# A chunked recurrent and attention block on one core: the layers' mixing and second feed-forward products in units of seven half-size products

## The chip, the core and the metric

The kernel runs on one core of one Trainium2 chip, as one program on its engines: TensorE (PE, with its weight loads PEld), VectorE (DVE), ScalarE (ACT), GpSimd (POOL) and SyncE (SP), which here starts the weight transfers. The metric is the device time of one execution in microseconds (us), the median of the runs given.

## What is computed

Two blocks follow each other on 512 tokens of width 1024, all in float32. The first (four recurrent mixers, a routed mixture of 32 experts with 4 per token, a gated embedding) is not touched. The second puts 16 extra rows ahead of the tokens (528 rows) and runs two layers of this form:

```python
for l in range(2):
    ...                                              # retention, pooling, forgetting attention -> o_r, o_p, o_f
    mix = jnp.concatenate([o_r, o_p, o_f], axis=-1)  # 528 x 1024
    mix = jnp.einsum('ble,ed->bld', mix, w_out)      # 1024 x 1024
    h = layer_norm(ALPHA * h + mix, ln1_g, ln1_b)
    a = jnp.einsum('bld,df->blf', h, w1)             # 1024 x 2816
    b = jnp.einsum('bld,df->blf', h, w3)
    y = jnp.einsum('blf,fd->bld', jax.nn.silu(a) * b, w2)   # 2816 x 1024
    h = layer_norm(ALPHA * h + y, ln2_g, ln2_b)
```

The last layer leaves the 16 extra rows out after attention, since the output is the 512 tokens.

## The kernel before

The second block is handled in row groups: "A" is the 16 extra rows (tile 0, called meta) and tiles 1 and 2 of 128 tokens, "B" is tiles 3 and 4. The order of the work on every engine is written out by hand in `layers()`: for each engine the same sequence of calls, `project` (the input products), `attend` (attention, a generator of 22 steps for A and 25 for B, one step at each `each(steps)`), `mix` (the product with `w_out`, then the first layer norm), `feed` (`feed_up`, the products with `w1` and `w3`, and `feed_down`, the product with `w2`, then the second layer norm). While the rows of one group go through `feed`, the attention steps of the next group are dealt out between its products. So `mix` of layer 0, B stands right behind the last `feed_down` of layer 0, A; `mix` of layer 1, A behind that of layer 0, B; and the second `feed_down` of layer 1, A behind `mix` of layer 1, B.

The 2816 inner features are 22 slices of 128, in two chunks of 12 and 10: `feed_up` fills `ff_t` with a chunk, `feed_down` multiplies it by its rows of `w2` and adds into the residual rows `h2`. `mix` and `feed_down` take for each of two column halves and each of two row tiles one product, 8, 12 or 10 slices deep, each slice a matmul of 128 columns by 512 (L1579, L1610), and one narrow product for the meta rows (L1570, L1613). Results go to a ring of three PSUM banks called `main`; DVE adds each to `h2` (L3129, L3191), and behind the last ones normalises the rows: statistics (L2746, L3153), aggregate (L2757, L3163), centre (L2760, L3166), reciprocal, scale (L2764, L3178), with a square root on ACT (L1869) between. PE needs from DVE only that a bank is free again, three results back. Weights come in pieces of 2 MB through a ring of four slots, in the order in which PE asks for them (`weights`).

## Time and profile before

| | |
|---|---|
| median of three runs | 3258.08 us (3255.95 to 3266.2) |
| span of the profiled execution | 3252.7 us, which is 3.25 us under the fastest of the three runs and 5.4 us under their median |
| the layers (from about 1750 us to the end) | 1502 us, PE busy 1482 us |
| mean granted TensorE clock | 0.973 of full speed |

The profile's span runs from the first to the last instruction; what a run's time holds beyond it is the start and end of the program. A program's matmul in float32 shows as two MATMUL records. A record's own time overlaps that of the next, so the pace of a series is read from its start and that of what follows.

### The profile page before, as it was taken

The page shows a single profiled execution, that of the slowest core. Times are in us where ns is not written, and L with a number is a line of the kernel's source. Part 1 is how long each engine was busy: PE and PEld are TensorE (multiplying, and loading weights), DVE is VectorE, ACT ScalarE, POOL GpSimd, SP SyncE. Part 2 cuts the span into 40 slices and gives each one's busy share as a digit, 9 for nine tenths or more (in the row PEclk, how much of TensorE's full clock was granted, in tenths as well). Part 3 has the DMA queues.
Part 4 walks back from the last instruction along what each step waited for, and adds up shares of the span by engine and source line. Part 5 has one row for each costly group of instructions (what it writes and reads, how often), then busy time and mean ns, then how long its engine had stood idle before and what let it go on. Part 6 is the DMA issues. An engine that isn't in the chain of part 4 may idle for free.

```text
span 3252.7 us, 52666 instructions
## 1 busy us (share of the span) xinstructions
PE 3120.2 (96%) x22631; PEld 1747.5 (54%) x22631; DVE 975.8 (30%) x2146; ACT 540.8 (17%) x1129; POOL 47.2 (1%) x58
## 2 busy tenths in 40 slices
PE   9878989999999999999999999999999999999999
PEld 3355545333343333333345668574785758675866
DVE  1633455232223223222363431223023122132101
ACT  1332311111111111111122220130102100040000
POOL 0000002000000000000010000000000000000000
PEclk9888979999999999999989999999999999999999
DMA  9800115999999999999863333234333243243532
GB/s 400 354 1 27 53 53 224 386 410 403 408 397 406 400 406 407 407 407 404 351 251 119 125 130 117 111 143 176 135 126 142 105 194 133 100 176 116 195 145 100
DMA packets 97466, 743.70 MB, mean 229 GB/s; under 512 B 11128, under 2 KB 38336, under 8 KB 57552
## 3 DMA queue, kind: packets, MB, share of 16 engines
q1 hardware_dynamic: 58768, 687.49, 53.6%
q10 hardware_dynamic: 32624, 30.52, 2.9%
q0 software_dynamic: 5968, 24.14, 1.9%
q8 instruction: 83, 1.36, 0.2%
q14 instruction: 23, 0.19, 0.0%
HBM read 674.98 MB, written 67.13 MB: 228 GB/s over the span
## 4 chain that ended last, share of the span: by engine, by line
PE 55%; DMA 28%; DVE 3%; ACT 2%; issue 1%; ACTq 1%; POOL 0%; DVEq 0%
DMA arena<-x_sorted 27%; PE psum L1593 19%; PE psum L1610 9%; PE psum L1540 5%; PE psum L1579 3%; PE psum L1551 3%; PE psum L1244 1%; PE psum L802 1%; ACTq L587 1%; PE psum L1355 1%; PE psum L820 1%; PE psum L1196 1%; PE psum L1319 1%; PE psum L1411 1%; PE psum L1457 1%
## 5 line engine op out<-in xcount | busy, mean ns | idle before, releaser
L1244 PE MATMUL psum<-weight_ring,arena 128*32 128x512 f32 x6192 | 680.8, 594 | 23.6 <-DVE arena L2862 21.7
L1593 PE MATMUL psum<-arena,weight_ring 128*128 128x256 f32 (+1 forms) x2816 | 632.2, 383 | 3.1 <-ACT arena L2226 3.1
L1593 PEld LDWEIGHTS psum<-arena,weight_ring 128*128 128x128 f32 x2816 | 527.6, 189 | 99.0 <-issue 11.0
L1244 PEld LDWEIGHTS psum<-weight_ring,arena 128*32 128x32 f32 x6192 | 199.7, 110 | 485.5 <-issue 464.3
L1319 PE MATMUL psum<-weight_ring,arena 128*32 128x256 f32 x6144 | 338.2, 380 | 0.0
L1610 PE MATMUL psum<-weight_ring 128*128 128x512 f32 x704 | 305.4, 593 | 4.2 <-DVE weight_ring L3149 4.2
L1319 PEld LDWEIGHTS psum<-weight_ring,arena 128*32 128x32 f32 x6144 | 196.6, 110 | 153.0 <-issue 26.8
L1610 PEld LDWEIGHTS psum<-weight_ring 128*128 128x128 f32 x704 | 132.9, 190 | 169.3 <-issue 162.5
L2884 DVE STREAM_TRANSPOSE arena<-arena 128x384 f32<-128x384 f32 x32 | 18.6, 580 | 630.8 <-DMA arena<-x_sorted 630.8
L3149 DVE TENSOR_TENSOR weight_ring<-weight_ring,psum 128x256 f32<-128x256 f32 (+1 forms) x88 | 37.5, 426 | 486.1 <-PE psum L1593 480.3
L1540 PE MATMUL psum<-weight_ring,arena 128*128 128x512 f32 (+2 forms) x512 | 170.0, 489 | 3.1 <-ACT arena L2226 3.1
L818 PE MATMUL psum<-arena,weight_ring 128*128 128x512 f32 x288 | 134.2, 617 | 10.9 <-DMA weight_ring<-weights 6.6
L1540 PEld LDWEIGHTS psum<-weight_ring,arena 128*128 128x128 f32 x512 | 96.0, 190 | 70.5 <-issue 59.8
L2273 ACT ACTIVATE weight_ring<-psum 128x256 f32<-128x256 f32 (+1 forms) x88 | 34.1, 387 | 513.2 <-PE psum L1593 513.0
L1551 PE MATMUL psum<-arena,weight_ring 128*128 128x272 f32 (+1 forms) x512 | 117.1, 387 | 0.0
L2103 ACT ACT_TABLE_LOAD x32 | 41.1, 1283 | 428.0 <-issue 428.0
L1579 PE MATMUL psum<-weight_ring,arena 128*128 128x512 f32 x256 | 110.6, 592 | 0.0
L1551 PEld LDWEIGHTS psum<-arena,weight_ring 128*128 128x128 f32 x512 | 95.9, 189 | 19.1 <-issue 2.0
L818 PEld LDWEIGHTS psum<-arena,weight_ring 128*128 128x128 f32 x288 | 54.5, 196 | 76.8 <-issue 67.2
L3191 DVE SCALAR_TENSOR_TENSOR arena<-arena,psum 128x512 f32<-128x512 f32 x32 | 22.1, 690 | 232.5 <-PE psum L1610 232.5
L820 PE MATMUL psum<-weight_ring,arena 128*128 128x512 f32 (+1 forms) x192 | 90.8, 601 | 0.0
L2109 ACT COPY arena<-psum 128x256 f32<-128x256 f32 x96 | 36.0, 375 | 293.2 <-PE psum L1319 280.0
(435 smaller groups left out, 2532.0 us busy)
## 6 DMA issues: line engine op xcount, KB each, us to landing
weight_ring<-exp_gu SPq DMA_DIRECT2D x129, 2048.0 KB, 11.9
weight_ring<-weights SPq DMA_DIRECT2D x104, 2048.0 KB, 7.8
weight_ring<-exp_down SPq DMA_DIRECT2D x64, 2048.0 KB, 11.5
x_sorted<-arena SPq DMA_DIRECT2D x2, 10752.0 KB
arena<-x_sorted ACTq DMA_DIRECT2D x132, 96.0 KB, 21.6
y_sorted<-arena ACTq DMA_DIRECT2D x128, 96.0 KB, 17.6
y_sorted<-arena SPq DMA_DIRECT2D x2, 5632.0 KB, 39.7
y_sorted<-arena SPq DMA_DIRECT2D x2, 5120.0 KB, 37.3
```

Of the source, the lines that this page charges most:

```text
L818: mm = pe.matmul(bank, w[:, k, a:a + P], x_t[:, k, :], start=(k == 0), stop=(k == KT - 1))
L820: mm = pe.matmul(bank[:, 0:width], x_t[:, k, t * P:(t + 1) * P], w[:, k, a:a + width], start=(k == 0), stop=(k == KT - 1))
L1244: mm = pe.matmul(psum[j * GROUP:(j + 1) * GROUP, g, :], xg[:, k // 4, g, k % 4 * GROUP:(k % 4 + 1) * GROUP], w[:, kk, j * 512:(j + 1) * 51 ...
L1319: mm = pe.matmul(psum[j * GROUP:(j + 1) * GROUP, 3 + g, 0:256], hid_t[:, g, k * GROUP:(k + 1) * GROUP], w[:, kk, j * 256:(j + 1) * 256], s ...
L1540: mm = pe.matmul(bank[:, 0:width], h2_t[:, k, OFF[t]:OFF[t] + P], w[:, k, 0:width], start=first, stop=last)
L1551: mm = pe.matmul(bank[:, 0:b - a], w[:, k, c:c + P], h2_t[:, k, a:b], start=first, stop=last)
L1579: mm = pe.matmul(bank, h2_t[:, k, OFF[t]:OFF[t] + P], ws[half][0][:, k, :], start=(k == 0), stop=(k == KT - 1))
L1593: mm = pe.matmul(bank[:, 0:b - a], w[:, k, col:col + P], h2_t[:, k, a:b], start=(k == 0), stop=(k == KT - 1))
L1610: mm = pe.matmul(bank, ff_t[:, f, OFF[t] - a:OFF[t] - a + P], w[:, half * 512:(half + 1) * 512], start=first, stop=last)
L2103: T.did(act.activation(sig[:, g, :], swi[:, g, 0:256], ACT.Sigmoid, scale=SWIGLU_ALPHA), swish_given)
L2109: T.did(act.copy(y_out[:, g, :], psum[:, 3 + g, 0:256]), y_drained)
L3149: V.did(dve.tensor_tensor(g, g, bank[:, 0:b - a], ALU.mult), main.drained["v"])
```

## The change

`mix` and `feed_down` become one function, `fast`, called 16 times (the list `FAST`). The features are cut in three chunks of 8, 8 and 6 slices instead of 12 and 10, so a unit has two row tiles (`t` and `first`), two column halves, and two halves of the depth of `depth` = 4 slices (3 in the last chunk). A unit makes its 2x2 blocks from seven products of `depth` matmuls where there were eight. For this, GpSimd forms the weight differences `b12 - b11` (in `fast_t1`) and `b22 - b12` (in place of b12), DVE forms four sums or differences of the left operand and two of the weights (`b11`, `b21` in place), ACT copies one product out of its bank, and DVE adds partial results together and to `h2`. The 16 meta rows keep their ordinary product, now ahead of the seven. One attention step stands ahead of the meta product and in each of the places 0, 2, 4 and 6 of a unit. The layer norm's parts of the last unit stand between and behind its additions. The lists of `layers()` keep their order with three chunks. Some buffers and semaphores move and a scratch area for GpSimd's transfers shrinks to 4096 bytes a partition to make room for the new tiles.

```diff
@@ -113,13 +113,27 @@
 ROW_CHUNKS = ((0, 512), (512, 512), (1024, 256), (1280, 256))
-FF_CHUNKS = ((0, 12), (12, FT))
+FF_CHUNKS = ((0, 8), (8, 16), (16, FT))
...
+FAST = [("mix", 0, "A", 0), ("down", 0, "A", 0), ("down", 0, "A", 1), ("down", 0, "A", 2),
+        ("mix", 0, "B", 0), ("down", 0, "B", 0), ("down", 0, "B", 1), ("down", 0, "B", 2),
+        ("mix", 1, "A", 0), ("down", 1, "A", 0), ("down", 1, "A", 1), ("mix", 1, "B", 0), ("down", 1, "A", 2),
+        ("down", 1, "B", 0), ("down", 1, "B", 1), ("down", 1, "B", 2)]
+STEP_SLOTS = (0, 2, 4, 6)
...
+    return KT // 2 if name == "mix" else (FF_CHUNKS[c][1] - FF_CHUNKS[c][0]) // 2
...
+            def fast(u, operand, ready, ready_late, steps):
+                name, l, x, c = FAST[u]
+                depth = fast_depth(name, c)
+                t, first = fast_tiles(x)
+                def rows(k, tile):
+                    return operand[:, k, OFF[tile] - operand_from(name, l, x):OFF[tile] - operand_from(name, l, x) + P]
+                def product(bank, lhs, rhs, start=True):
+                    for k in range(depth):
+                        mm = pe.matmul(bank, lhs(k), rhs[:, k, :], start=start and k == 0, stop=(k == depth - 1), skip_group_check=True)
+                    return mm
+                at = W_OUT if name == "mix" else W_DOWN + 2 * c
+                wa, at_a = weights(l, at)
+                if has_meta(l, x):
+                    wb, at_b = weights(l, at + 1)
+                    ready()
+                    ready_late(META)
+                    if name == "down":
+                        each(steps)
+                    bank = main.bank(pe)
+                    for k in range(2 * depth):
+                        w = (wa, wb)[k // depth].rearrange("p k n -> p (k n)").rearrange("p (k n) -> p k n", k=4)[:, k % depth, :]
+                        for j in range(4):
+                            mm = pe.matmul(bank[32 * j:32 * j + META, 0:256], operand[:, k, 0:META], w[:, j * 256:(j + 1) * 256],
+                                           start=(k == 0), stop=(k == 2 * depth - 1), skip_group_check=True)
+                    main.ship(mm, ("fast", u, "meta"), "v")
+                    fast_meta[u] = main.done()
+                else:
+                    ready()
+                    at_b = None
+                if 0 in STEP_SLOTS:
+                    each(steps)
+                bank_p1 = main.reserve(pe, 0)
+                if at_b is None:
+                    fast_at[u] = (at_a, at_a + 1)
+                else:
+                    fast_at[u] = (at_a, at_b)
+                b11, b12, b21, b22 = fast_views(u)
+                product(bank_p1, lambda k: rows(k, t), b11).then_inc(part_filled, 1)
+                if 1 in STEP_SLOTS:
+                    each(steps)
+                bank_p7 = main.reserve(pe, 2)
+                pe.wait_ge(sums_ready, 8 * u + 2)
+                pe.wait_ge(diffs_ready, 3 * u + 3)
+                product(bank_p7, lambda k: rows(k, first), b12).then_inc(part_filled, 1)
+                if 2 in STEP_SLOTS:
+                    each(steps)
+                if at_b is None:
+                    wb, at_b = weights(l, at + 1)
+                    assert at_b == at_a + 1
+                ready_late(P)
+                pe.wait_ge(part_copied, u + 1)
+                mm = product(bank_p1, lambda k: rows(depth + k, t), b21, False)
+                main.ship(mm, ("fast", u, "c11"), "v")
+                if 3 in STEP_SLOTS:
+                    each(steps)
+                bank_p6 = main.reserve(pe, 0)
+                pe.wait_ge(sums_ready, 8 * u + 5)
+                mm = product(bank_p6, lambda k: fast_s2[:, k, :], b11)
+                main.ship(mm, ("fast", u, "p6"), "v")
+                if 4 in STEP_SLOTS:
+                    each(steps)
+                bank_p5 = main.reserve(pe, 1)
+                product(bank_p5, lambda k: fast_s1[:, k, :], fast_t1).then_inc(part_filled, 1)
+                if 5 in STEP_SLOTS:
+                    each(steps)
+                pe.wait_ge(sums_ready, 8 * u + 7)
+                mm = product(bank_p7, lambda k: rows(depth + k, first), b21, False)
+                main.ship(mm, ("fast", u, "c21"), "v")
+                piece_free[at_a] = main.done()
+                if 6 in STEP_SLOTS:
+                    each(steps)
+                pe.wait_ge(sums_ready, 8 * u + 8)
+                mm = product(bank_p5, lambda k: fast_s4[:, k, :], b22, False)
+                main.ship(mm, ("fast", u, "c12"), "v")
+                piece_free[at_b] = main.done()
...
+            def differences(u):
+                name, l, x, c = FAST[u]
+                depth = fast_depth(name, c)
+                b11, b12, b21, b22 = fast_views(u)
+                if u:
+                    pool.wait_ge(part_filled, 3 * u)
+                at_a, at_b = fast_at[u]
+                pool.wait_ge(layer_landed[at_a % LAYER_SLOTS], layer_count(at_a))
+                pool.tensor_tensor(fast_t1[:, 0:depth, :], b12, b11, ALU.subtract).then_inc(diffs_ready, 1)
+                pool.wait_ge(diffs_ready, 3 * u + 1)
+                pool.wait_ge(layer_landed[at_b % LAYER_SLOTS], layer_count(at_b))
+                if u in fast_meta:
+                    pool.wait_ge(*fast_meta[u])
+                for part in (slice(0, depth // 2), slice(depth // 2, depth)):
+                    pool.tensor_tensor(b12[:, part, :], b22[:, part, :], b12[:, part, :], ALU.subtract).then_inc(diffs_ready, 1)
...
+                for n in range(7):
+                    if n in STEP_SLOTS:
+                        each(steps)
+                    if n == 0:
+                        act.wait_ge(part_filled, 3 * u + 1)
+                        A.did(act.copy(fast_u2, main.peek(("fast", u, "c11"))), part_copied)
...
+                    dve.wait_ge(*main.drained_of(("mix", l, t)))
+                V.settle()
+                fast(FAST.index(("mix", l, x, 0)), h2_t, iter(()), sem("mid_ready"), landed)
...
+                V.settle()
+                then(dve.tensor_tensor(s1, rows(0, first), rows(1, first), ALU.add), sums_ready)
+                V.did(dve.tensor_tensor(rows(0, first), rows(0, t), rows(0, first), ALU.subtract), sums_ready)
+                then(dve.tensor_tensor(s2, s1, rows(0, t), ALU.subtract), sums_ready)
+                V.did(dve.tensor_tensor(s4, rows(1, t), s2, ALU.subtract), sums_ready)
+                if 0 in STEP_SLOTS:
+                    each(steps)
+                dve.wait_ge(diffs_ready, 3 * u + 3)
+                dve.wait_ge(part_filled, 3 * u + 1)
+                then(dve.tensor_tensor(b11, b22, t1, ALU.subtract), sums_ready)
+                if 1 in STEP_SLOTS:
+                    each(steps)
+                if 2 in STEP_SLOTS:
+                    each(steps)
+                add(t, 0, main.take(dve, ("fast", u, "c11")), scale, main.drained["v"])
+                V.did(dve.tensor_tensor(b21, b21, b11, ALU.subtract), sums_ready)
+                if ready is not None:
+                    V.settle_other(main.drained["v"])
+                    half_stats(t, 0)
+                if 3 in STEP_SLOTS:
+                    each(steps)
+                bank = main.take(dve, ("fast", u, "p6"))
+                dve.wait_ge(part_copied, u + 1)
+                then(dve.tensor_tensor(fast_u2, fast_u2, bank, ALU.add), main.drained["v"])
+                dve.wait_ge(part_filled, 3 * u + 2)
+                then(dve.tensor_tensor(fast_u3, fast_u2, main.peek(("fast", u, "c21")), ALU.add), sums_ready)
+                add(t, 1, fast_u2, scale)
+                add(first, 0, fast_u2, scale)
+                add(first, 1, fast_u3, scale)
+                V.settle()
+                if 4 in STEP_SLOTS:
+                    each(steps)
+                dve.wait_ge(part_filled, 3 * u + 3)
+                add(first, 1, main.peek(("fast", u, "c12")), 1.0, sums_ready)
+                if ready is not None:
+                    V.settle()
+                    half_stats(first, 1)
+                if 5 in STEP_SLOTS:
+                    each(steps)
+                add(first, 0, main.take(dve, ("fast", u, "c21")), 1.0, main.drained["v"])
+                if ready is not None:
+                    V.settle()
+                    dve.wait_ge(sem("layer_ln_landed"), 16 * landed)
+                    half_stats(first, 0)
+                    centered = norm_centered(first)
+                if 6 in STEP_SLOTS:
+                    each(steps)
+                add(t, 1, main.take(dve, ("fast", u, "c12")), 1.0, main.drained["v"])
+                V.settle()
+                if ready is not None:
+                    norm_scaled(centered, ready, parts)
+                    half_stats(t, 1)
+                    norm_scaled(norm_centered(t), ready, parts)
+                    if has_meta(l, x):
+                        half_stats(0, 0)
+                        half_stats(0, 1)
+                        norm_scaled(norm_centered(0), ready, parts)
+
```

Three places show what the engines now run. First PE at `mix` of layer 0, B, right behind the last `feed_down` of layer 0, A. Before, L1613 is the narrow product of the down unit, L1579 the mix:

```order
L1613 MATMUL psum<-weight_ring 16x256 [waits main_drained_dve]
L1613 MATMUL psum<-weight_ring 16x256 x39
L1579 MATMUL psum<-weight_ring,arena 128x512 [waits fox_outs_drained,layer_weights_landed_1,main_drained_act,main_drained_dve,fox_turns_drained_dve,fox_turns_drained_act]
L1579 MATMUL psum<-weight_ring,arena 128x512 x6
L1579 MATMUL psum<-weight_ring,arena 128x512 [waits fox_outs_drained]
L1579 MATMUL psum<-weight_ring,arena 128x512 [waits main_drained_dve]
L1579 MATMUL psum<-weight_ring,arena 128x512 x7
L1579 MATMUL psum<-weight_ring,arena 128x512 [waits main_drained_dve,layer_weights_landed_2]
L1579 MATMUL psum<-weight_ring,arena 128x512 x7
L1579 MATMUL psum<-weight_ring,arena 128x512 [waits main_drained_dve]
L1579 MATMUL psum<-weight_ring,arena 128x512 x7
```

And with the change, the last rows of the unit of depth 3 and the first of the mix unit (L1620 is every product of a unit):

```order
L1620 MATMUL psum<-weight_ring 128x512 [waits fast_sums_ready]
L1620 MATMUL psum<-weight_ring 128x512 x2
L1620 MATMUL psum<-weight_ring,arena 128x512 [waits fast_sums_ready]
L1620 MATMUL psum<-weight_ring,arena 128x512 x2
L1620 MATMUL psum<-weight_ring,arena 128x512 [waits main_drained_act,fox_turns_drained_dve,main_drained_dve,fox_turns_drained_act,start_landed_1]
L1620 MATMUL psum<-weight_ring,arena 128x512 x3
L1620 MATMUL psum<-weight_ring,arena 128x512 [waits fast_diffs_ready,fast_sums_ready,main_drained_dve]
L1620 MATMUL psum<-weight_ring,arena 128x512 x3
L1620 MATMUL psum<-weight_ring,arena 128x512 [waits fast_part_copied,fox_outs_drained,start_landed_2]
L1620 MATMUL psum<-weight_ring,arena 128x512 x3
```

The second product of the mix unit now waits for DVE's sums and GpSimd's differences; before, a mix product waited for a free bank only.

Second, DVE at the same place, with the change. L3332 are additions to `h2`, L3292 to L3314 the layer norm, L3343 and L3344 the first two sums of the mix unit, which let PE's second product go:

```order
L3314 SCALAR_TENSOR_TENSOR arena<-arena 128x1024 [waits vector_step]
L3292 BN_STATS arena<-arena 128x6 [waits layer_start]
L3299 BN_AGGR arena<-arena 128x2 [waits vector_step]
L3302 SCALAR_TENSOR_TENSOR arena<-arena 128x1024 [waits variance_ready]
L3311 RECIPROCAL arena<-arena 128x1 [waits root_ready]
L3314 SCALAR_TENSOR_TENSOR arena<-arena 128x1024 [waits vector_step]
L3292 BN_STATS arena<-arena 16x6 [waits layer_start]
L3292 BN_STATS arena<-arena 16x6
L3299 BN_AGGR arena<-arena 16x2 [waits vector_step]
L3302 SCALAR_TENSOR_TENSOR arena<-arena 16x1024 [waits variance_ready]
L3311 RECIPROCAL arena<-arena 16x1 [waits root_ready]
L3314 SCALAR_TENSOR_TENSOR arena<-arena 16x1024 [waits vector_step]
L3343 TENSOR_TENSOR arena<-arena 128x512 [waits layer_start,main_drained_act]
L3344 TENSOR_TENSOR arena<-arena 128x4x128 [waits fast_sums_ready]
```

The norms of tile 1 (scale), tile 2 and the meta rows stand ahead of the sums that the mix unit begins with; before, no sums followed.

Third, PE in the second down unit of layer 1, A, with the change, from place 4 on (the last of these rows begins the product behind it). L1509, L854, L1537 and L1544 are an attention step:

```order
L1620 MATMUL psum<-weight_ring,arena 128x512 x3
L1509 MATMUL psum<-weight_ring,arena 64x128 [waits fox_outs_drained,fox_turns_drained_act]
L1509 MATMUL psum<-weight_ring,arena 64x128 x9
L854 MATMUL psum<-arena,weight_ring 16x128 [waits fox_turns_drained_act,fox_weights_ready]
L854 MATMUL psum<-arena,weight_ring 128x128 x3
L854 MATMUL psum<-arena,weight_ring 16x128 [waits fox_turns_drained_act]
L854 MATMUL psum<-arena,weight_ring 128x128 x3
L1537 MATMUL psum<-arena 128x512 [waits score_drained_dve]
L1537 MATMUL psum<-arena 128x512
L1544 MATMUL psum<-arena 128x16 [waits fox_turns_drained_act] x2
L1620 MATMUL psum<-arena 128x512 [waits main_drained_dve]
```

A step that waits for `fox_weights_ready` (DVE's work on the scores of the step before) now stands two products of 4 matmuls behind that step; before, two of 8 or one of 12 or 10.

## Rows read from the trace of the kernel before

**Rows 1.** Page: share of the span; 40 slices, tenths busy.
```profile
PE 3120.2 (96%) x22631; PEld 1747.5 (54%) x22631; DVE 975.8 (30%) x2146; ACT 540.8 (17%) x1129; POOL 47.2 (1%) x58
...
PEclk9888979999999999999989999999999999999999
```
**Rows 2.** Windows of the layers: busy us of each engine (count), granted clock, DMA.
```profile
1950.00:2240.00 290.00, 287.68 (x1382) 198.15 (x1385) 72.59 (x139) 51.91 (x99) 0.00 (x0) 1.00 0.30 113
2240.00:2350.00 110.00, 109.63 (x639) 68.76 (x632) 21.18 (x35) 12.85 (x41) 1.06 (x2) 1.00 0.50 192
sum 1502.00, PE 1482.30 PEld 1022.16 DVE 365.10 ACT 235.99 POOL 2.66; mean PE 211.76 PEld 146.02 DVE 52.16 ACT 33.71 POOL 0.38
```
**Rows 3.** PE's timeline around a mix: start, us, instruction, count [idle before].
```profile
1902.04 27.63 PE L1579 MATMUL psum<-weight_ring,arena 128*128 128x512 f32 x64
1929.60 3.69 PE L1570 MATMUL psum<-weight_ring,arena 128*16 128x128 f32 x128
...
2201.73 34.60 PE L1610 MATMUL psum<-weight_ring 128*128 128x512 f32 x80 [0.53 <-DVE weight_ring L3149]
2236.26 4.51 PE L1613 MATMUL psum<-weight_ring 128*16 128x256 f32 x80
```
**Rows 4.** DVE groups in the layers by shape: count, busy us, mean ns.
```profile
L3191 DVE SCALAR_TENSOR_TENSOR arena<-arena,psum 128x512 f32<-128x512 f32 x32 | 22.1, 690 | 232.5 <-PE psum L1610 232.5
L3061 DVE TENSOR_TENSOR weight_ring<-psum,weight_ring 128x1024 f32<-128x1024 f32 x6 | 7.3, 1225 | 10.0 <-PE psum L1485 10.0
L2942 DVE TENSOR_TENSOR arena<-arena 128x384 f32<-128x384 f32 x8 | 4.5, 558 | 0.3
L3195 DVE SCALAR_TENSOR_TENSOR arena<-arena,psum 16x256 f32<-16x256 f32 x8 | 3.3, 416 | 4.9 <-PE psum L1613 4.6
```
**Rows 5.** GpSimd groups of the whole span.
```profile
L1799 POOL COPY arena<-arena 128x1024 f32<-128x1024 f32 x4 | 4.2, 1061 | 530.7 <-DVE arena L2764 530.7
```
**Rows 6.** DVE's timeline, norm of tile 2 and the meta rows.
```profile
2237.17 0.69 DVE L3153 BATCH_NORM_STATS2 arena<-arena 128x6 f32<-128x512 f32 x1
2237.90 0.21 DVE L3163 BATCH_NORM_AGGREGATE arena<-arena 128x2 f32<-128x12 f32 x1
2238.14 1.29 DVE L3166 SCALAR_TENSOR_TENSOR arena<-arena 128x1024 f32<-128x1024 f32 x1
2239.54 1.29 DVE L3178 SCALAR_TENSOR_TENSOR arena<-arena 128x1024 f32<-128x1024 f32 x1
2242.71 1.27 DVE L3153 BATCH_NORM_STATS2 arena<-arena 16x6 f32<-16x512 f32 x2
```
**Rows 7.** Timeline of one attention step's chain, 2112 to 2121 us.
```profile
2113.11 1.13 PE L1485 MATMUL psum<-arena 64*128 64x512 f32 x4
2114.29 1.23 DVE L3061 TENSOR_TENSOR weight_ring<-psum,weight_ring 128x1024 f32<-128x1024 f32 x1 [1.51 <-PE psum L1485]
2119.24 0.90 DVE L3084 TENSOR_SCALAR weight_ring<-weight_ring,arena 128x528 f32<-128x528 f32 x2
```
**Rows 8.** PE's timeline in the first block, between two idle times.
```profile
1654.82 1.58 PE L802 MATMUL psum<-arena 128*128 128x128 f32 x8 [2.70 <-DVE arena L2902]
1676.85 1.98 PE L1340 MATMUL psum<-weight_ring,arena 128*128 128x512 f32 x4 [2.28 <-DVE arena L2917]
```
**Rows 9.** Windows of 5 us around these.
```profile
1640.00:1645.00 5.00, 5.00 (x6) 1.41 (x5) 2.07 (x3) 0.00 (x0) 3.76 (x4) 0.50 0.97 408
...
1655.00:1660.00 5.00, 4.32 (x12) 2.37 (x12) 3.94 (x6) 4.04 (x5) 3.82 (x4) 0.53 1.02 406
1660.00:1665.00 5.00, 5.00 (x11) 2.14 (x10) 4.89 (x5) 0.00 (x0) 0.00 (x0) 0.79 0.71 284
1675.00:1680.00 5.00, 3.15 (x8) 1.48 (x9) 4.45 (x7) 1.49 (x2) 0.00 (x0) 1.00 0.62 203
```
**Rows 10.** Timeline of the end of the kernel.
```profile
3245.72 0.69 DVE L3191 SCALAR_TENSOR_TENSOR arena<-arena,psum 128x512 f32<-128x512 f32 x1 [4.16 <-PE psum L1610]
3248.81 1.42 DVE L3178 SCALAR_TENSOR_TENSOR arena<-arena 128x512 f32<-128x512 f32 x2
```

264 lines of the change are left out of this document (130 added, 134 removed).

## The prediction

> **What bounds the kernel now.** The page comes first: PE is busy 96% of the span, DVE 30%, POOL 1%, and the granted clock of TensorE is at its upper level in almost all slices behind the first block [rows 1]. The windows of the layers say the same of the part that is changed: 1482 of 1502 us busy at clock 1.00, with DVE at 365 us and POOL at 2.7 us [rows 2]. So in the layers the time is PE's work, and what PE waits for there now is about 20 us, some 6 of them behind its last product. PE's timeline shows that the work is dense: the 64 records of the mix of layer 0, A take from 1902.04 to 1929.60 us, 27.56 us or 0.431 us a record, and the 80 records of a down chunk from 2201.73 to 2236.26, again 0.431, across four banks and without idle time; idle time stands only ahead of the first, 0.53 us, where PE waits for DVE's last product into `ff_t` [rows 3]. A matmul 128 by 512 in float32 is two records, so 0.861 us.
>
> **What is taken away.** Twelve units have depth 4 (four mixes, eight down chunks), four have depth 3. Each makes seven products of its depth where there were eight, so 12 x 4 + 4 x 3 = 60 matmuls or 120 records go: 120 x 0.4306 = 51.7 us. The narrow meta products hold the same columns: a mix had 128 records of 128 columns in 3.7 us, now 64 of 256, and a record of 256 takes 4.51 / 80 = 0.056 us, 3.6 us [rows 3]. Nothing gained there.
>
> **What a plain unit costs on the other engines.** DVE had four additions of 0.69 us. Now it has, at depth 4, four sums of 512 elements, two of 2048 and nine additions. An operation on 384 elements takes 0.56 us and one on 1024 takes 1.23, a slope of 1.04 ns an element [rows 4], so 512 take 0.69 and 2048 take 2.29 us (an estimate from these rows). The sum is 4 x 0.69 + 2 x 2.29 + 9 x 0.69 = 13.6 us, against 28 x 0.861 = 24.1 us of PE. It fits in total; what counts is each hand-over. With t = 0 at PE's first product and 3.45 us a product: the two sums for the second product are ready at 1.5 (needed 3.45); b11 at 5.9, behind the first product (needed 10.3); DVE takes the third product at 10.5, then b21 until 13.5, and the fourth at 14.0, so `fast_u3` is there at 15.4 (needed 17.2); the addition of the fifth ends at 18.1 (needed 20.7). None is late. At depth 3 a product is 2.58 us, and with the statistics of 0.69 us between [rows 6] `fast_u3` comes at 12.4 (needed 12.9) and the last sum at 15.2 (needed 15.5): just in time, with no room. GpSimd's differences are made while `feed_up` runs, where POOL is idle. I book nothing for the hand-overs; if each of the four units of depth 3 missed both by 0.5 us, that would be 4 us.
>
> **What comes on the path.** (a) The norms. At three places a unit follows directly behind one that ends in a layer norm, and its second product needs two sums that stand behind all of it in DVE's order. From the rows, statistics 0.69, aggregate 0.21, centre until scale 1.40, scale 1.29 and gaps make 3.8 us for a tile, and 4.3 for the meta rows, whose two statistics take 1.27 [rows 6]. Behind the end of PE's last product in layer 0, A, DVE needs 1.65 for the last addition (it comes late from the centring), 1.5 for the scale of the first tile, 3.8, 4.3, and 1.5 for the two sums: 12.75 us. PE covers 3.45 with its first product: 9.3 us idle at mix 0, B. At mix 1, A there are no meta rows behind: 5.0. At the last down chunk of layer 1, A, behind mix 1, B, it is 0.9 + 1.5 + 3.8 + 1.2 = 7.4 less 2.6: 4.8. Together 19.1 us. The cover that these norms had, PE's products into three banks, is what the new wait removes.
> (b) The meta units. The differences for b12 may start only behind the meta product, and the second product needs them. No row has a GpSimd operation with two inputs. The nearest is its copy of 1024 elements, 1.06 us [rows 5]; below, two such pieces take 2.1 us and hide under the 3.45; above, I take each input at a copy's time, 2.12 us a piece, 4.7 with hand-overs, so 1.3 us idle, and 1.0 at depth 3 (pieces of 512 and 1024). I take the upper end, since two operands must be read: 2.3 us for the two meta units that have no attention step to cover it. Both ends differ by 2 us only.
> The Trainium skill, "GPSIMD Engine Reference", section "Elementwise — side-by-side cycle accounting", gives 4497 ns for a `tensor_tensor` of 2048 float32 elements against 2293 ns on DVE. By that the two waits would be 2.9 us and not 2.3. No run shows the former yet; the latter agrees with 2.29 from the slope of rows 4.
> (c) Attention steps. A step's scores end at 2114.24 on PE, DVE and ACT work on them until 2120.14, 5.9 us [rows 7], and the step after it needs the result. `feed_up` has two products of 3.8 us and PE's own part of a step, 2.5 us, between, so it hides there. In a unit two products of 3.45 stand between, but DVE puts its sums ahead of the step. Where heavy steps fall in a unit (steps 21 to 23 in the second chunk of layer 0, A, and 20 to 23 in that of layer 1, A), I get 1.7 + 1.0 and 1.4 us. The other units with steps hold light ones, under 1 us of DVE each: nothing. Together 4.1 us.
> (d) A third chunk adds four waits at a chunk's start of 0.53 us [rows 3]: 2.1.
> (e) The end. From DVE's last addition at 3245.72 to its last scale at 3250.23 are 4.5 us [rows 10]. Now the scale of the first tile and the late last addition stand in between: 2.4 more.
> (f) The clock. Behind an idle time of 2.70 us at 1652 us the granted clock shows 0.53 and 0.79 in two windows of 5 us, that is the lower level, 1.2 GHz, for some 6 us; behind one of 2.28 us it stays at 1.00 [rows 8, 9]. The first costs 5 x 0.47 + 5 x 0.21 = 3.4 us of full speed, about 3.2 of it outside the wait. I take that for each of the three waits of (a), 9.6 us, and none for those under 2 us. Below: nothing. Above: 12 us at the lower level as at 1640 us [rows 9], 6 us each.
> The sum is -51.7 + 19.1 + 2.3 + 4.1 + 2.1 + 2.4 + 9.6 = **-12.1 us**. The span is 3252.7 us, so 3240.6; its difference to the median, 5.4 us, stays, and the median goes from 3258.1 to **3246 us**. The likeliest case's own range is 3237 to 3255.
>
> **The rivals.** Waits and clock are mild (chance 0.2): no drop of the clock behind waits of 5 us, and part of the norm hidden; -51.7 + 30.0 = -21.7 or a little under, 3236 us. For it speaks that the clock at 1.00 survived 2.28 us; against it that 2.70 us did not.
> The clock turns it round (0.14): each of the seven waits, the short ones too, is followed by 12 us at the lower level, as the window at 1640 us has it behind a row of short gaps. 7 x 6 = 42 in place of 9.6: -51.7 + 30.0 + 42 = +20, 3278 us. It decides from 3.1 us a wait on (21.7 / 7). Against it: in the layers PE is dense on both sides of each wait.
> The two engines collide (0.12): GpSimd's differences run beside DVE's sums with two inputs in the meta units and at the norms. If both took twice as long there, b12 would come some 4.5 us later in two units and the sums and norms at mix 0, B and mix 1, A about 2 us later: +11 to +13, so no change, 3259 us. The profile has no moment at which both work on such operations. The Trainium skill, "GPSIMD Engine Reference", section "Key points", says that GpSimd shares its SBUF interfaces with VectorE and contends with DVE instructions with two SBUF inputs; it gives no size.
> More waits than I see (0.09): the hand-overs in the units of depth 3 and the step units cost 1 us each in 10 units, 3256 us.
>
> **How the numbers follow.** My own case has 0.45. This measurement can't tell a change under about 0.3%, 9.8 us: faster is under 3248.3, slower over 3267.9. My case ends faster in about three of four (0.34 of 0.45), the rest within; the mild one is faster (0.2); the collision and the added waits lie within, with a fifth of them on either side; the clock case is slower. That makes faster 0.56, same 0.27, slower 0.17. The range runs from under the mild case, 3230, to 3272, which leaves out most of the clock case and a tail below.
>
> **What will show it.** L1620 with 28 x 12 + 21 x 4 = 420 matmuls, 840 records at 0.431 us, where L1579 and L1610 had 960. PE idle ahead of the second product at mix 0, B by 9 us, at mix 1, A and the last chunk of 1, A by 5, released by DVE's L3344; the granted clock behind them. POOL's L1953 at 2.1 us or 2.3 a piece. DVE's L3351 at 2.29 us. I am wrong if PE is idle for more than 35 us more than before in the layers (then the hand-overs are not hidden), or for less than 20 (then the norms are covered by something that I missed).

## The result, and the profile after

The changed kernel takes 3276.81 us (median of 11 runs, 3271.49 to 3284.14) against 3264.88 us for the kernel before, run beside it: a ratio of 1.0043, 95% interval 1.0033 to 1.0054. It is 0.43% slower, some 14 us (the two medians alone are 11.9 us apart, 0.37%). The forecast was 3246 us. Of the 30.8 us between forecast and measurement, 6.8 are the kernel before itself, which took 3264.88 us beside the changed one and 3258.08 us in the three runs that the forecast started from.

The first rows of the page of the changed kernel (its profiled execution spans 3282.3 us), which answer to [rows 1]:

```profile
PE 3083.7 (94%) x22447; PEld 1726.7 (53%) x22447; DVE 1186.1 (36%) x2338; ACT 551.2 (17%) x1146; POOL 190.5 (6%) x106
...
PEclk9888889899999999999989999998999999999999
```

PE has 36.5 us less to do over the whole span, and the kernel is slower. The windows from the layers' first load to the end, first of the kernel before and then of the changed one (length, busy us of PE, PEld, DVE, ACT and POOL with counts, granted clock, DMA), split that:

```profile
1740.40:3252.70 1512.30, 1491.90 (x6919) 1026.82 (x6917) 365.10 (x748) 237.16 (x563) 8.56 (x17) 1.00 0.37 138
```
```profile
1751.60:3282.30 1530.70, 1467.12 (x6735) 1012.90 (x6733) 575.80 (x940) 247.87 (x580) 149.15 (x65) 0.98 0.37 136
```

The layers are 18.4 us longer in this pair of profiles. PE's idle time in them went from 20.4 us (1512.30 less 1491.90) to 63.6: **+43.2**, where 30.0 was forecast. PE's busy time fell by 24.8 us and not by 51.7: at most 26.9 us of what was removed was given back to a lower clock, where 9.6 was forecast (the granted clock, weighed by PE's busy time in windows of 0.5 us, gives 25.2). 43.2 and 26.9 less 51.7 make 18.4.

PE's timeline of the changed kernel (start, us, instruction, count, idle time before it) through the end of the last unit of layer 0, A and through mix 0, B, where most of this lies:

```profile
2243.16 7.08 PE L1620 MATMUL psum<-weight_ring 128*128 128x512 f32 x12 [2.10 <-DVE weight_ring L3344]
2250.09 2.74 PE L1620 MATMUL psum<-weight_ring,arena 128*128 128x512 f32 x6
...
2261.64 9.05 PE L1620 MATMUL psum<-weight_ring,arena 128*128 128x512 f32 x14 [3.66 <-DVE arena L3332]
2279.05 13.16 PE L1620 MATMUL psum<-weight_ring,arena 128*128 128x512 f32 x24 [8.36 <-issue]
2292.05 3.60 PE L1620 MATMUL psum<-arena 128*128 128x512 f32 x8
```

The 8.36 us ahead of mix 0, B's second product are the norm wait that was forecast at 9.3. The 3.66 us were not forecast at all. Six records take 2.74 us at the full clock, and the 12 behind the first wait take 7.08 where two such groups would take 5.4. The windows of 5 us there show the clock fall to its lower level (0.50 of 2.4 GHz is 1.2 GHz) behind each of these waits:

```profile
2260.00:2265.00 5.00, 3.36 (x4) 1.51 (x5) 4.83 (x7) 0.29 (x1) 4.92 (x3) 0.54 0.88 364
...
2275.00:2280.00 5.00, 0.95 (x1) 0.50 (x2) 4.67 (x7) 0.40 (x1) 0.56 (x1) 0.50 0.19 67
2280.00:2285.00 5.00, 5.00 (x8) 2.09 (x7) 2.48 (x2) 0.00 (x0) 0.00 (x0) 0.57 0.34 143
2285.00:2290.00 5.00, 5.00 (x13) 2.19 (x12) 1.11 (x2) 0.00 (x0) 0.00 (x0) 1.00 0.00 0
```

What kept PE waiting for 3.66 us stands in the timelines of POOL and of DVE, here around the twin of that wait in layer 0, B:

```profile
2631.28 4.83 POOL L1947 TENSOR_TENSOR arena<-weight_ring 128x2048 f32<-128x2048 f32 x1 [29.91 <-PE psum L1620]
...
2636.18 4.98 POOL L1953 TENSOR_TENSOR weight_ring<-weight_ring 128x1024 f32<-128x1024 f32 x2
```
```profile
2631.66 4.99 DVE L3332 SCALAR_TENSOR_TENSOR arena<-arena,weight_ring 128x512 f32<-128x512 f32 x1
2636.69 0.69 DVE L3332 SCALAR_TENSOR_TENSOR arena<-arena,psum 128x512 f32<-128x512 f32 x1
2637.41 0.70 DVE L3292 BATCH_NORM_STATS2 arena<-arena 128x6 f32<-128x512 f32 x1
...
2639.70 2.55 DVE L3302 SCALAR_TENSOR_TENSOR arena<-arena 128x1024 f32<-128x1024 f32 x1
```

An addition of 512 elements that takes 0.69 us elsewhere took 4.99. It began 0.4 us behind POOL's subtraction and ended at 2636.65, half a microsecond behind POOL's end at 2636.11. The next, with its second input in PSUM, and the statistics, with one input, run at their own time although POOL is busy again; the centring, which reads two inputs from SBUF (1.29 us in [rows 6]), again takes 2.55, and ends 1.1 us behind POOL's second piece. The same thing reaches out of the units: POOL's first difference is released as soon as its weights land, 50 us ahead of the first unit, and falls on an attention step:

```profile
1863.06 4.51 POOL L1947 TENSOR_TENSOR arena<-weight_ring 128x2048 f32<-128x2048 f32 x1 [105.56 <-DMA weight_ring<-weights]
```
```profile
1863.97 3.65 DVE L3225 TENSOR_TENSOR weight_ring<-weight_ring,arena 16x32 f32<-16x32 f32 x1
```
```profile
1871.41 1.36 PE L854 MATMUL psum<-arena,weight_ring 16*16 16x16 f32 x6 [2.65 <-DVE weight_ring L3235]
```

That addition of 16 by 32 took 0.18 us in the kernel before:

```profile
1852.72 0.18 DVE L3074 TENSOR_TENSOR weight_ring<-weight_ring,arena 16x32 f32<-16x32 f32 x1
```

In the changed kernel it ends at 1867.62, POOL's instruction at 1867.57, and PE stands idle for 2.65 us that were not there.

Outside the layers the two programs do the same work, but the two profiled executions differ by 11.2 us where the layers begin. The last issue of the scatter on POOL and the first load of sorted rows on ACT are 7.1 us apart before and 27.6 in the changed kernel's profile; here both engines' timelines of the latter:

```profile
563.71 0.96 POOL L1911 DMA_INDIRECT x_sorted<-arena  x1 [0.30 <-issue]
```
```profile
591.33 1.85 ACTq L613 DMA_DIRECT2D arena<-x_sorted  x4
```

So the study had three questions: what holds DVE, what the low clock costs, and whether the scatter belongs to the change (the compile argument for the scratch area was changed with it, and the prediction gave it no price).

### The profile page after: what moved, and what is told of

Same layout as the page of the kernel before. It is cut to its first block, busy times and chain, and to the rows that moved or that the text cites. A ratio compares the mean times of both kernels' runs of the same rounds, so it can differ in the third digit from the quotient of the medians.

```text
span 3282.3 us, 52707 instructions
## 1 busy us (share of the span) xinstructions
PE 3083.7 (94%) x22447; PEld 1726.7 (53%) x22447; DVE 1186.1 (36%) x2338; ACT 551.2 (17%) x1146; POOL 190.5 (6%) x106
## 4 chain that ended last, share of the span: by engine, by line
PE 51%; DMA 28%; DVE 6%; issue 2%; ACT 2%; ACTq 1%; POOL 1%; DVEq 0%
DMA arena<-x_sorted 26%; PE psum L1713 19%; PE psum L1620 10%; PE psum L1592 5%; PE psum L1603 3%; PE psum L854 1%; PE psum L1296 1%; PE psum L1371 1%; PE psum L1407 1%; ACTq L613 1%; PE psum L1248 1%; PE psum L872 1%; PE psum L1463 1%; DMA x_sorted<-arena 1%; PE psum L1509 1%
## 5 line engine op out<-in xcount | busy, mean ns | idle before, releaser
L1620 PE MATMUL psum<-weight_ring,arena 128*128 128x512 f32 x368 | 176.6, 632 | 22.3 <-issue 12.6
L1620 PE MATMUL psum<-weight_ring 128*128 128x512 f32 x352 | 162.7, 611 | 11.3 <-issue 8.6
L1620 PEld LDWEIGHTS psum<-weight_ring,arena 128*128 128x128 f32 x368 | 73.8, 203 | 118.1 <-issue 108.3
L1592 PEld LDWEIGHTS psum<-weight_ring,arena 128*128 128x128 f32 x512 | 96.0, 190 | 70.5 <-issue 59.8
L1947 POOL TENSOR_TENSOR arena<-weight_ring 128x2048 f32<-128x2048 f32 (+1 forms) x16 | 68.6, 4286 | 1033.1 <-DMA weight_ring<-weights 958.3
L1620 PEld LDWEIGHTS psum<-weight_ring 128*128 128x128 f32 x352 | 66.9, 194 | 95.9 <-issue 94.8
```

Of the source, the lines that this page charges most:

```text
L1592: mm = pe.matmul(bank[:, 0:width], h2_t[:, k, OFF[t]:OFF[t] + P], w[:, k, 0:width], start=first, stop=last)
L1620: mm = pe.matmul(bank, lhs(k), rhs[:, k, :], start=start and k == 0, stop=(k == depth - 1), skip_group_check=True)
L1947: pool.tensor_tensor(fast_t1[:, 0:depth, :], b12, b11, ALU.subtract).then_inc(diffs_ready, 1)
```

## The experiments

Ratios are to the kernel before, on the same chip; 1 to 4, 5 to 8, 9 with 10, and 11 were run beside it on four occasions. The changed kernel gave 1.0043 and 1.0042 on two of them, the two edits of 4 gave 0.9948 and 0.9962, so a difference of 0.15% between ratios of two occasions says little. "Layers" is the time from the layers' first load to the end of the span, in one profile each; in two executions of one program it differs by some 3 us (1530.7 and 1528.1, 1497.1 and 1499.7), and between the two kernels without the units that differ only in the scratch area by 4.7.

**1. The scratch area alone.**

```diff
-    nc = bacc.Bacc("TRN2", target_bir_lowering=False, num_devices=1)
+    nc = bacc.Bacc("TRN2", target_bir_lowering=False, num_devices=1, dynamic_dma_scratch_size=4096)
```

> The kernel before with one argument changed: the compile argument that sets the scratch area for software-made DMA descriptors to 4096, as in the changed kernel; no instruction moves. Theory A (the smaller area makes the scatter of the sorted rows land late): from the first of the 16 indirect issues to the first load of sorted rows about 48 us instead of 27.8, and the kernel 15 to 21 us (0.45 to 0.65 %) slower than before. Rival B (the scatter's 20.6 us in the changed kernel's trace have another cause, such as where the expert weights' loads fell in that run): about 28 us again, and the time within 0.3 % of before.

Measured: 0.9989 (0.9976 to 1.0002). The first load of sorted rows came 27.75 us after the first indirect issue (547.00 to 574.75). Theory A is wrong. The changed kernel profiled once more (experiment 5) has 27.8 us as well. In 13 profiles, nine of them with the small area and the changed units, the 48 us occur once; what caused them there stays open, and the change is not it. Where the layers begin varies by more than that wait would explain: between 1732.4 and 1751.6 us over these profiles, and at 1749.1 in experiment 5 without it. The layers of this run are 1517.0 us with 20.4 us idle, as before; the 4 us between them are the clock. It dipped at two places where it had not in the profile of before, once behind the very wait of 2.18 us that stands in both, once behind one of 0.70 us that stands in both. So some 4 us of a difference between two profiles can be that.

**2. POOL's differences in short instructions.**

```diff
-                pool.tensor_tensor(fast_t1[:, 0:depth, :], b12, b11, ALU.subtract).then_inc(diffs_ready, 1)
+                for k in range(depth):
+                    last = pool.tensor_tensor(fast_t1[:, k:k + 1, :], b12[:, k:k + 1, :], b11[:, k:k + 1, :], ALU.subtract)
+                last.then_inc(diffs_ready, 1)
...
-                for part in (slice(0, depth // 2), slice(depth // 2, depth)):
-                    pool.tensor_tensor(b12[:, part, :], b22[:, part, :], b12[:, part, :], ALU.subtract).then_inc(diffs_ready, 1)
+                for k in range(depth):
+                    last = pool.tensor_tensor(b12[:, k:k + 1, :], b22[:, k:k + 1, :], b12[:, k:k + 1, :], ALU.subtract)
+                last.then_inc(diffs_ready, 2)
```

> The changed kernel, with the weight differences on POOL cut into instructions of 512 columns (four of them, or three, where one had 2048 or 1536). Theory A (a DVE instruction whose inputs are both in SBUF does not start until the POOL instruction that is running has ended, so its length is what hurts): the DVE instruction that took 3.65 us instead of 0.18 ahead of the first unit, and the three additions that took 6.20 us instead of 2.1 in the last unit of a feed, come down to little more than their own time; PE's wait of 2.65 us at the first difference and its two of 3.66 us go, with the low clock behind the first; 8 to 16 us faster than the changed kernel as it is. Rival B (POOL holds the DVE off across consecutive instructions as well, or both run slower side by side in proportion): the same total hold, no gain, within 3 us of the changed kernel or slower by the added instructions.

Measured: 0.9983 (0.9967 to 0.9999), some 0.6% under the changed kernel. The layers take 1509.8 us, 20.9 less than in the changed kernel's profile; 57.2 of them idle, 6.4 less, and 1452.6 busy, 14.5 less. The POOL and DVE timelines of this kernel at the first difference:

```profile
1851.74 5.13 POOL L1948 TENSOR_TENSOR arena<-weight_ring 128x512 f32<-128x512 f32 x4 [105.44 <-DMA weight_ring<-weights]
```
```profile
1852.66 0.38 DVE L3228 TENSOR_TENSOR weight_ring<-weight_ring,arena 16x32 f32<-16x32 f32 x1
...
1853.18 1.33 DVE L3228 TENSOR_TENSOR weight_ring<-weight_ring,arena 128x256 f32<-128x256 f32 x1
```

DVE gets in between two pieces: the hold is 0.2 and 0.9 us (1.33 against 0.40) instead of 3.5, and both 3.66 us waits and the 2.65 us one are gone. Theory A holds, and the gain is above the 8 to 16 us that it gave. The four pieces take 5.13 us instead of 4.51, which nothing waits for here. Most of the gain is the clock: short waits went, and with them the slow products behind them. What grew is the norm waits, since PE now arrives earlier at them: 10.32, 6.82 and 5.63 us at the three places, 22.8 in all against 19.0.

**3. The sums ahead of the norm.** The four activation sums of mix 0B, mix 1A and down 1A chunk 2 are called from within the unit before, ahead of its `norm_scaled`:

```diff
+                if u + 1 in EARLY:
...
+                    fast_sums(u + 1)
                 if ready is not None:
                     norm_scaled(centered, ready, parts)
```

> The changed kernel, with the four activation sums of the units that follow a norm (mix 0B, mix 1A, down 1A chunk 2) computed ahead of the rest of that norm. Theory A (the norms of the unit before are what keeps PE waiting there): PE's idle times of 8.36, 4.26 and 6.33 us ahead of those units' second products go, and with them the low clock of the products around them (13 us for 24 records instead of 10.3); 15 to 20 us faster than the changed kernel. Rival B (the norm then ends 2 to 3 us later, and the row transposes that read it are late instead): less than half of that comes back, the rest stands as a longer wait at the start of the next projection or of the next feed.

Measured: 0.9994 (0.9982 to 1.0007), 16 us under the changed kernel. The layers take 1514.6 us, 53.3 idle. Theory A holds in the main, though not all the waits go: mix 0, B's second product no longer waits, but ACT's copy does, since it is queued behind the square roots of the same norm. PE's timeline of this kernel:

```profile
2242.10 12.46 PE L1621 MATMUL psum<-weight_ring,arena 128*128 128x512 f32 x22 [3.66 <-DVE arena L3348]
2258.77 5.46 PE L1621 MATMUL psum<-weight_ring,arena 128*128 128x512 f32 x6 [4.21 <-ACT weight_ring L2417]
```

So 8.36 became 4.21 there; at mix 1, A 0.84 us are left of 4.26, and at the last chunk of 1, A 1.47 and 0.90 of 6.33. The hold of 3.66 us is untouched.

**4. Both edits.**

> The changed kernel with both edits: POOL's differences in instructions of 512 columns, and the sums of three units ahead of the norm's rest. If both theories A hold and their gains add, 25 to 35 us faster than the changed kernel, near 3245 us; if either rival B holds, what the other edit alone gives. The scatter's 20 us stay in either case, if they come from the scratch area.

Measured: 0.9948 (0.9929 to 0.9966), 3240.93 us. They nearly add: 0.95% under the changed kernel, where the edits alone gave 0.60 and 0.49. The layers take 1497.1 us, 33.6 less than in the changed kernel, 48.5 idle. This is within the 25 to 35 us that both theories A gave. What now stands ahead of the second product at mix 0, B and mix 1, A is POOL, whose short pieces and DVE's sums keep each other waiting (four pieces take 7.14 us there instead of 5.13, and three of DVE's four sums 1.63 to 1.75 us instead of 0.69); PE's timeline of this kernel:

```profile
2246.41 4.07 PE L1621 MATMUL psum<-weight_ring,arena 128*128 128x512 f32 x5 [3.90 <-POOL weight_ring L1956]
```

**5. The changed kernel again.**

> The changed kernel once more, unaltered, with a new profile. Theory A (the scatter's 48 us from the first indirect issue to the first load of sorted rows belong to that one execution): about 28 us in this profile, a span near 3270, and the layers again 18 us longer than before; the ratio to before stays at 1.004. Rival B (something in the changed program makes it so in each execution): 48 us again.

Measured: 1.0042 (1.0026 to 1.0059). The layers take 1528.1 us with 63.9 idle, so the layers' part of the result repeats, and the scatter's does not. One of the waits that the hold makes did not bring the low clock this time; PE's timeline and the windows behind it (granted clock 1.00 in both):

```profile
1870.31 0.93 PE L854 MATMUL psum<-arena,weight_ring 16*16 16x16 f32 x6 [2.46 <-DVE weight_ring L3235]
```
```profile
1870.00:1875.00 5.00, 4.69 (x25) 3.57 (x26) 2.13 (x5) 4.26 (x13) 0.00 (x0) 1.00 0.86 360
1875.00:1880.00 5.00, 5.00 (x39) 3.69 (x38) 3.13 (x11) 1.42 (x7) 0.00 (x0) 1.00 0.25 56
```

**6. Three more edits at the same three units.** In PE the order of the second and third product is turned round at these units, ACT's copy goes ahead of the roots, and the meta rows' norm of layer 0 goes behind mix 0B's weight difference:

```diff
+                if u not in EARLY:
+                    second()
...
                 main.ship(mm, ("fast", u, "c11"), "v")
+                if u in EARLY:
+                    second()
...
+                    if u + 1 in EARLY:
+                        copy_first(u + 1)
...
+                if u == 4:
+                    half_stats(0, 0)
+                    half_stats(0, 1)
+                    norm_scaled(norm_centered(0), sem("layer_start"))
```

> Both edits (POOL's differences in instructions of 512 columns; the sums of three units ahead of the norm) and three more at those units: PE takes the product that needs no weight difference second, ACT's copy of the first product stands ahead of the square roots of the norm, and the norm of the meta rows of layer 0 follows behind mix 0B's last weight difference. Theory A (PE's 3.90 us for POOL, 2.61 us for ACT and 0.82 us for DVE in mix 0B, 3.89 us in mix 1A, and 1.46 and 0.90 us in down 1A chunk 2 are the order of three queues, and nothing else is late behind them): 6 to 11 us faster than with the two edits alone, near 0.992 of before. Rival B (the wait moves: the meta rows' norm is late for the next projection, or the second product waits for POOL all the same): less than 4 us.

Measured: 0.9965 (0.9952 to 0.9979), so no gain over the two edits alone. The waits named are gone, but 4.26, 4.25 and 2.08 us came in their place ahead of the next product. DVE's timeline of this kernel says who is late, the sum of weights (L3383) that stands behind the second tile's norm:

```profile
2264.01 1.29 DVE L3334 SCALAR_TENSOR_TENSOR arena<-arena 128x1024 f32<-128x1024 f32 x1
2265.60 2.29 DVE L3383 TENSOR_TENSOR weight_ring<-weight_ring,arena 128x2048 f32<-128x2048 f32 x1 [0.30 <-DVE arena L3334]
```

Rival B, in a form of its own: the wait moved by one product.

**7. A third chunk with ordinary products.** The kernel before, with `FF_CHUNKS = ((0, 8), (8, 16), (16, FT))` and two weight pieces a chunk.

> The kernel before with nothing but the feed-forward chunks changed: three of 8, 8 and 6 blocks instead of 12 and 10, each with the ordinary product, and the attention steps spread over them. Theory A (a third chunk costs little: a wait of about 0.6 us at its start in four feeds, and an add more per chunk on a DVE that is not the bound): 2 to 4 us slower than before, within 0.3 %. Rival B (the attention steps bunch at the new borders and cost waits as they do in the changed kernel, 4.4 us ahead of the second unit of layer 0 and 5.0 in layer 1): 8 to 12 us slower; then the third chunk and not the half-size products accounts for most of what the scheme failed to give.

Measured: 1.0013 (1.0001 to 1.0025); layers 1515.2 us, 20.9 idle. Theory A: the third chunk costs 3 to 4 us by these two numbers, and not the 8 to 12 of rival B. Of the layers' 2.9 us, 1.7 are a drop of the clock that the other profile lacks.

**8. One POOL instruction in the kernel before**, with the small scratch area, and a buffer of its own that POOL clears at the start.

```diff
+                if free is None:
+                    at = mark["mix"]
+                    pool.wait_ge(sem("zeros_ready"), 2)
+                    pool.wait_ge(layer_landed[at % LAYER_SLOTS], 16 * (at // LAYER_SLOTS + 1))
+                    pool.tensor_tensor(spare[:, 0:2048], spare[:, 0:2048], spare[:, 0:2048], ALU.subtract)
```

> The kernel before (with the scratch area of 4096) and one POOL instruction more, a subtraction of 128x2048 on a buffer of its own that nothing reads, released when mix 0A's first weights have landed, where the changed kernel has its first weight difference. Theory A (a DVE instruction whose inputs are both in SBUF is held until POOL's has ended): the 16x32 DVE addition that is due beside it takes up to 3.7 us instead of 0.18, PE waits 2 to 3 us behind it and runs slower for some 10 us: 3 to 6 us more up to mix 0A (0.1 to 0.2 %). Rival B (it was not the instruction but the weights it read, which PE or a transfer used as well): no DVE instruction longer than before, no wait.

Measured: 1.0016 (1.0005 to 1.0027), against 0.9989 for the same kernel without the instruction, on another occasion. Its POOL, DVE and PE timelines:

```profile
1850.66 3.59 POOL L1839 TENSOR_TENSOR spare<-spare 128x2048 f32<-128x2048 f32 x1 [105.42 <-DMA weight_ring<-weights]
```
```profile
1851.51 2.79 DVE L3082 TENSOR_TENSOR weight_ring<-weight_ring,arena 16x32 f32<-16x32 f32 x1
```
```profile
1858.10 0.92 PE L803 MATMUL psum<-arena,weight_ring 16*16 16x16 f32 x6 [1.60 <-DVE weight_ring L3092]
```

POOL's instruction ends at 1854.25, the addition at 1854.30, for 0.18 us of work. Nothing else reads its buffer, so rival B (the weights that it read) is out: the instruction itself holds DVE. PE waited 1.60 us, less than the 2 to 3 expected, and the window of 5 us behind it shows the clock at 0.70, 1.5 us more: 3 us in all, the lower end of what theory A gave. That this dip belongs to the wait isn't shown: the profile of experiment 1, without the instruction, has one of the same size some 15 us later in the layers, and both profiles' layers take 1517.0 us. So what experiment 8 shows is the hold and the wait, and not what they cost.

**9. The sum of weights ahead of the second norm**, on top of 6.

> The kernel of e6_best with one thing moved: at its three units the sum of weights that the third product reads (it stood behind the second tile's norm on DVE) stands ahead of that norm. In e6_best PE waited 4.26, 4.25 and 2.08 us for it. Theory A (DVE's order is all that was late): these go, and nothing else comes in their place: 7 to 10 us faster than e6_best, 5 to 8 faster than the two edits alone. Rival B (the norm that is now 2.3 us later, or the halves of the norm's rows that the turn of rows reads, makes the next projection wait): under 4 us faster than e6_best.

Measured: 0.9947 (0.9929 to 0.9966), 3236.9 us; layers 1493.0 us, 45.2 idle, the shortest of all. The waits of 6 went in mix 1A (4.25 to 0.85) and in down 1A (2.08 to 0.73), while mix 0B kept 4.64 us, for the addition that is queued behind the meta rows' norm. Compared with 6 the layers are 7.8 us shorter, within the 7 to 10 of theory A; but only 2.2 of it are idle time, and 3.4 are two drops of the clock in the profile of 6, behind waits of 0.69 and 2.55 us that stand in both and left the clock up in 9. So the edit is worth less than theory A had.

**10. The two edits once more, on the same chip as 9.**

> The kernel of e4_both once more, beside e9_wsum on one chip. The layers from their first product to their last should again take 1326 us (what the order of the queues sets repeats to a microsecond), and the ratio to before again about 0.995; if the ratio moves by more than 0.3 %, the difference between e4_both and e6_best is one between chips and says nothing of their edits.

Measured: 0.9962 (0.9949 to 0.9974). From the first product of the first unit to the last product of the last one 1328.9 us, against 1326.1 in experiment 4. The ratio moved by 0.14%, under the 0.3% that the expectation had set. The interval overlaps that of 9; that 9 is better than 4 is read from the layers (1493.0 against 1497.1 and 1499.7, of which 45.2 against 48.5 and 47.0 idle) and not from the ratios, and is 2 to 3 us besides the clock.

**11. The meta rows' norm later still.**

```diff
                 add(first, 0, main.take(dve, ("fast", u, "c21")), 1.0, main.drained["v"])
+                if u == 4:
+                    half_stats(0, 0)
+                    half_stats(0, 1)
+                    norm_scaled(norm_centered(0), sem("layer_start"))
```

> The kernel of e9_wsum with the norm of layer 0's meta rows put later inside mix 0B: behind the last addition of the third result instead of behind the weight difference. In e9_wsum it takes 4.3 us of DVE at 2263 and PE waits 4.64 us for the addition queued behind it. Theory A (that norm can hide in the gap that DVE has ahead of the last result): the 4.64 us go and mix 0B with the chunk ahead of it takes 52 to 53 us instead of 56.95; 3 to 5 us faster than e9_wsum. Rival B (the next projection's turn of the meta rows waits for it): a wait of 2 us or more at the start of the projection of layer 1, and less than 3 us gained.

Measured: 0.9978 (0.9963 to 0.9994), and layers of 1506.3 us with 55.0 idle: a loss against 9. The 4.64 us went and the stretch took 51.3 us, as theory A has it. But the loader of the next norm's parameters waits for this norm, and its transfer lands 10 us after the issue. The POOL, DVE and PE timelines of this kernel:

```profile
2274.56 0.56 POOL L1944 DMA_DIRECT2D arena<-ln_mid  x1 [22.08 <-DVE arena L3334]
```
```profile
2272.79 1.27 DVE L3334 SCALAR_TENSOR_TENSOR arena<-arena 16x1024 f32<-16x1024 f32 x1
2284.51 0.69 DVE L3312 BATCH_NORM_STATS2 arena<-arena 128x6 f32<-128x512 f32 x1 [10.45 <-DMA arena<-ln_mid]
```
```profile
2287.52 2.90 PE L855 MATMUL psum<-arena 128*128 128x128 f32 x16 [13.97 <-DVE arena L3374]
```

Neither theory had this: rival B looked for a wait in the right place, but for another reason.

The layers of all profiles by their windows (us, one profile each; the last column is the clock's shortfall from 1.00, summed over windows of 5 us):

| kernel | layers | PE busy | PE idle | clock lost |
|---|---|---|---|---|
| before | 1512.3 | 1491.9 | 20.4 | 1.7 |
| 1, small scratch area | 1517.0 | 1496.6 | 20.4 | 5.5 |
| 7, three plain chunks | 1515.2 | 1494.3 | 20.9 | 3.6 |
| 8, one POOL instruction | 1517.0 | 1495.1 | 21.9 | 5.8 |
| changed / again (5) | 1530.7 / 1528.1 | 1467.1 / 1464.2 | 63.6 / 63.9 | 33.1 / 29.7 |
| 2, short POOL instructions | 1509.8 | 1452.6 | 57.2 | 17.8 |
| 3, sums ahead of the norm | 1514.6 | 1461.3 | 53.3 | 23.6 |
| 4 / 10, both | 1497.1 / 1499.7 | 1448.6 / 1452.8 | 48.5 / 47.0 | 7.7 / 12.8 |
| 6, three more edits | 1500.8 | 1453.4 | 47.4 | 11.1 |
| 9, sum of weights early | 1493.0 | 1447.8 | 45.2 | 5.9 |
| 11, meta norm later | 1506.3 | 1451.3 | 55.0 | 16.2 |

Over the two profiles of either kernel the units make the layers 11 to 18 us longer (1528.1 and 1530.7 against 1512.3 and 1517.0), which agrees with the 14 us of the result.

## Why the prediction was wrong

The direction was wrong, and by its own terms two steps failed.

**The step that failed first: the place of the collision between the two engines.** The prediction held it as a rival at 0.12, priced at 11 to 13 us, looked for it in the meta units and at the norms, and let both engines take twice as long. What the runs show is no sharing but a hold: a DVE instruction with both inputs in SBUF does not get through until POOL's instruction ends, whatever its own size (0.18 us became 3.65, and 2.79 in experiment 8). So its price goes by the length of POOL's instruction (holds of 3.5 and 4.3 us beside instructions of 4.51 and 4.83), and it strikes wherever POOL happens to start. The differences "made while `feed_up` runs, where POOL is idle" were booked at nothing because POOL was idle; DVE was not. At 1863 us it hit an attention step. In the two feeds of layer 0 the next mix's difference started beside the last additions of the depth 3 unit (3.66 us each). In the second chunk of 0, A, PE's wait for an attention step was 3.87 us, and 1.71 once POOL's instructions were short, so about the 1.7 forecast was the step's own and the rest the hold. The Trainium skill, "SBUF — State Buffer", section "Who interferes with whom", states that the contention is an exclusive lock, that a DVE instruction with two SBUF inputs contends with a GpSimd instruction that reads SBUF, and that one with at most one SBUF input (outside of DVE's two-port modes) does not. The trace agrees, with the addition of 4.99 us and the one beside it, from PSUM, at 0.69. The prediction had cited only the page that gives no size, and made the collision proportional. By experiment 2, which only cuts POOL's instructions, the holds cost 0.6% or about 20 us; by the profiles 6.4 us of idle time (10 to 12 us of waits less, the norm waits 3.8 longer) and 14.5 of busy time.

**The second: (f), the clock.** It booked 3.2 us behind each of three waits and none for the others. Low clock shows behind ten: 2.65, 2.33, 3.87, 2.10, 3.66, 8.36, 3.66, 4.26, 6.33 and 2.76 us, each with 1.7 to 5.1 us of full speed lost, 3.1 in the mean, 30.7 in all, 25.2 of it in PE's busy time. The price was about right and the number of waits was not: seven of the ten are the holds, the meta units and the last feed, which the sum had at nothing or under 2 us. How long the wait is doesn't settle it alone. In the layers of all thirteen profiles, each of the 36 waits of 2.75 us or more was followed by a stretch at the lower clock; of the 20 between 2.0 and 2.7 us nine were and eleven were not, the same wait of the same program among both (2.46 us in experiment 5, 2.65 in the first profile; 2.10 us in both); and five more such stretches began behind waits of 0.51 to 0.70 us, and one behind 1.60. This is the rival in which the clock turns it round, with its direction right, and its price per wait twice what was measured, for more waits than it had; that its 3278 us lie next to the 3276.81 is luck. About half of the loss fell out of the first failure: with the holds gone (2) it is 17.8 us, with the norms out of the way too (4) 7.7, or 12.8 in the second profile (10). Of the 33.6 us between the changed kernel and experiment 4, 15.1 are idle time and 18.5 are products that ran faster.

**What held.** (a) The norms: 8.36, 4.26 and 6.33 us, together 18.95, against 9.3, 5.0 and 4.8, together 19.1. Experiment 3 shows that this is DVE's order, and that the same norm also holds ACT's copy. (e) The end: from PE's last product to the end 7.1 us before (the prediction read some 6) and 9.0 after, +1.9 against 2.4. (d) The third chunk: experiment 7 gives about 3 us against 2.1. The plain units of depth 4 have no hand-over waits: the first two units of the last feed take 24.28 us each to the end of their last record, against 24.1 in the working. So the prediction's own sign, more than 35 us of added idle time, did come true, but not for the reason that it gave there (hand-overs inside the units that are not hidden). The 51.7 us are there nearly whole: in experiment 9 PE's busy time is 44.1 us less, and the clock took 3.2 back in busy time, so 47.3 were removed; in the changed kernel 24.8 and 25.2 make 50.0. The rest was not traced.

**Terms that were mis-sized.** (b) The two meta units cost 2.33 and 2.10 us, 4.4 against 2.3. POOL's pieces of 1024 take 2.41 us in the mean, above the upper end of 2.12 that was taken, but in the second the hold also stands in it (DVE's first sum took 2.33 us instead of 0.56). (c) In 1, A the attention step cost 0.32 us, not 1.4. A wait at the start of the last feed grew from 1.11 to 2.76 us; it was not in the list, and its cause was not traced.

So the sum as it should have read: some 50 removed; 30 us of waits as forecast, some 13 more, 12 of them holds of DVE by POOL; and 25 us, not 9.6, for products at a lower clock. That makes +18 for this pair of profiles.

**The better version.** Both edits together beat both kernels (0.9948 and 0.9962 in two measurements: 12 to 17 us under the kernel before, 26 to 31 under the changed one), and experiment 9 is by its layers a little better again, at 0.9947. All of these are gains of about half a per cent or less. The scheme is worth it here once POOL's instructions are short and no norm stands between two units.

## What to carry to other kernels

Work that is given to an idle engine is free only if it shares nothing with a busy one: look at what DVE has with both inputs in SBUF over the whole stretch in which POOL may run, not at POOL's own idle time, and cut POOL's elementwise instructions short where they meet (here 512 elements, at 0.6 us more for 2048). Where PE is dense on both sides of a new wait of 2.75 us or more, price it at its length and 1.7 to 5.1 us of slow products behind it, 3 in the mean; between 2 and 2.75 us that came about every other time here. When an edit removes a wait, name the next thing in that queue: three times here (3, 6 and 11) the wait came back one product later or from another queue, once through a parameter load nobody had on the list.

## What the hardware showed beyond this

A DVE instruction with both inputs in SBUF that comes while POOL's runs is held to its end whatever DVE's size, and gets in between two back-to-back POOL instructions. POOL is slowed in turn: its pieces of 512 columns take 1.28 us alone (5.13 for four), and 2.2 in the mean (8.84 for four, experiment 2) beside the norm's centring and scaling on DVE, which have both inputs in SBUF. A subtraction of 128x2048 on one buffer, with both inputs and the output the same, took POOL 3.59 us, one with two inputs in different places 4.51; why they differ was not looked into. And in experiment 11 a transfer of norm parameters (1 MB) took 10 us from its issue on POOL to the DVE instruction that it released, which makes it a poor thing to have behind a late event.
